# Late norms of a 14-part transformer kernel: the sum of squares moved from GpSimd to VectorE, formed by fp32r products, and placed behind the third weight slab in the FFNs

## The reference

```
y = x * rsqrt(mean(x * x) + 1e-6) * g
x = x + rms_norm(sq_relu_mlp(rms_norm(x, g2), w1, w2), g3)      # mlp
x = x + 0.5 * (silu(h @ w_gate) * (h @ w_up)) @ w_down          # ffn, h = rms_norm(x)
```

## Time and profile before

| what | value |
|---|---|
| median of 3 runs | 2957.7 us (2955.51 to 2959.45) |
| the profiled execution's own time | 2941.98 us |
| its span | 2940.2 us |
| PE busy | 2802.9 us (95%) |
| DVE busy | 1695.6 us (58%) |
| ACT busy | 1352.6 us (46%) |
| POOL busy | 131.6 us (4%), of it L464 54.7 us in 30 operations |
| chain that ended last | PE 86%, ACT 6%, DVE 6%, POOL 1%, issue 1% |
| mean granted TensorE clock | 0.984 |

### The profile page before, as it was taken

One profiled execution on the slowest core, in us unless ns is written; L12 is line 12 of the kernel. 1 busy time (PEld: TensorE's weight loads), 2 busy tenths in 40 slices (PEclk: granted clock), 3 DMA queues, 4 the chain that ended last, 5 costly groups with the idle time before them and its releaser, 6 DMA issues.

```text
span 2940.2 us, 50425 instructions
## 1 busy us (share of the span) xinstructions
PE 2802.9 (95%) x22436; PEld 2707.9 (92%) x22436; DVE 1695.6 (58%) x1997; ACT 1352.6 (46%) x1621; POOL 131.6 (4%) x123
## 2 busy tenths in 40 slices
PE   7999999999998999989999999899999999799998
PEld 7888998899997999989999999889999999789998
DVE  6766644465465654865655654754664654755564
ACT  4634534454436543553544445454544444454443
POOL 1200000000000000200000000000000000000000
PEclk9999999999999999999999999899999999899999
DMA  6402554355442554511555655324665655324563
GB/s 188 152 20 73 189 185 134 110 158 186 158 158 72 169 190 129 158 58 44 158 187 155 190 187 166 108 87 144 180 188 178 187 187 162 97 95 163 159 200 115
DMA packets 426633, 427.95 MB, mean 146 GB/s; under 512 B 8275, under 2 KB 397761, under 8 KB 426289
## 3 DMA queue, kind: packets, MB, share of 16 engines
q1 hardware_dynamic: 426064, 424.37, 46.2%
q0 software_dynamic: 352, 0.36, 0.1%
HBM read 423.65 MB, written 1.05 MB: 144 GB/s over the span
## 4 chain that ended last, share of the span: by engine, by line
PE 86%; ACT 6%; DVE 6%; POOL 1%; issue 1%; DMA 0%; SPq 0%; POOLq 0%; ACTq 0%; DVEq 0%
PE ps L476 85%; ACT wH L1189 2%; DVE hL L1726 1%; DVE wL L1702 1%; POOL sq L464 1%; PE ps L819 1%; DVE sq L1753 1%; DVE xT L1756 1%; ACT hidden_parts L1233 1%; DMA ring<-in_gdn_w_in 0%; ACT L1202 0%; ACT sq L1228 0%; PE ps L957 0%; DVE hidden_parts L1726 0%; DVE arena L2170 0%
## 5 line engine op out<-in xcount | busy, mean ns | idle before, releaser
L1702 DVE TENSOR_TENSOR wL<-ring,wH 128x2048 fp32r<-128x2048 f32 x400 | 916.9, 2292 | 876.7 <-ACT wH L1189 876.2
L1189 ACT ACTIVATE wH<-ring 128x2048 fp32r<-128x2048 f32 x400 | 766.7, 1917 | 1203.4 <-PE ps L476 1187.2
L476 PE MATMUL ps<-hidden_parts,wH 128*128 128x256 f32 x6784 | 1031.6, 280 | 8.2 <-ACT hidden_parts L1233 3.1
L476 PEld LDWEIGHTS ps<-hidden_parts,wH 128*128 128x128 f32 x6784 | 930.9, 189 | 11.9 <-issue 4.3
L476 PE MATMUL ps<-hidden_parts,wL 128*128 128x256 f32 x3392 | 712.0, 280 | 0.3 <-DVE wL L1702 0.2
L476 PEld LDWEIGHTS ps<-hidden_parts,wL 128*128 128x128 f32 x3392 | 535.9, 189 | 0.7 <-DVE wL L1702 0.7
L476 PE MATMUL ps<-hH,wH 128*128 128x256 f32 x2624 | 377.3, 286 | 8.8 <-ACT hH L1223 4.7
L476 PE MATMUL ps<-hL,wH 128*128 128x256 f32 x2624 | 357.8, 283 | 10.0 <-DVE hL L1726 10.0
L476 PE MATMUL ps<-hH,wL 128*128 128x256 f32 x2624 | 361.5, 279 | 1.6 <-DVE wL L1702 1.6
L476 PEld LDWEIGHTS ps<-hH,wH 128*128 128x128 f32 x2624 | 336.7, 191 | 23.0 <-issue 22.0
L476 PEld LDWEIGHTS ps<-hL,wH 128*128 128x128 f32 x2624 | 331.7, 192 | 11.6 <-DVE hL L1726 11.6
(11 more groups left out here) (262 smaller groups left out, 2030.6 us busy)
## 6 DMA issues: line engine op xcount, KB each, us to landing
ring<-in_mlp_w SPq DMA_DIRECT2D x128, 1024.0 KB, 5.3
ring<-in_ffn_w_gate SPq DMA_DIRECT2D x88, 512.0 KB, 4.0
ring<-in_ffn_w_up SPq DMA_DIRECT2D x88, 512.0 KB, 5.3
ring<-in_ffn_w_down SPq DMA_DIRECT2D x44, 1024.0 KB, 4.9
ring<-in_gdn_w_in SPq DMA_DIRECT2D x32, 1024.0 KB, 5.6
ring<-in_w_in SPq DMA_DIRECT2D x28, 1024.0 KB, 5.3
ring<-in_mlstm_w_in SPq DMA_DIRECT2D x12, 1024.0 KB, 5.3
ring<-in_diff_w_in SPq DMA_DIRECT2D x12, 1024.0 KB, 5.1
```

Of the source, the lines that this page charges most:

```text
L476: return pe.matmul(o, l, r, start=start, stop=stop, **k)
L1189: f(wH[:, n % PARTS, :], ring[:, n % RING, :], ACT.Copy).then_inc(sem("high_split"), 1)
L1702: tt(wL[:, n % PARTS, :], ring[:, n % RING, :], wH[:, n % PARTS, :].bitcast(F32), ALU.subtract)\
```

## The change

GpSimd's three additions go. DVE makes them, in `late_low`, behind its low split of slab 1, each waiting for the one before; then it splits the sum into fp32r halves `sumH`, `sumL` (two operations of 256 columns), laid into chunks 8 and 9 of the low hidden half. TensorE forms the sum over the partitions with two fp32r products. `ones` becomes an fp32r tile, filled by a memset of `rs_mem` and a copy on GpSimd at the start. In the MLP the floor is split likewise: ACT copies the high half behind the last hidden group, DVE subtracts the low half, TensorE adds two fp32r products. In the FFN `summed_norm` stands behind slab 2 (the third slab) and no longer behind `first_products`.

```diff
@@ gpsimd, start and loop over the parts
-            pool.memset(ones[:, :], 1.0)
+            W.chain(pool.memset(rs_mem[:, :], 1.0))
+            pool.tensor_copy(onesR[:, :], rs_mem[:, :])
...
-                if kind in LATE:
-                    pool.wait_ge(sem("xsq_ready"), W.next("xsq_ready", 4))
-                    for n in (4, 2, 1):
-                        ins = pool.tensor_tensor(sq[:, 0:n, :], sq[:, 0:n, :], sq[:, n:2 * n, :], ALU.add)
-                        if n > 1:
-                            W.chain(ins)
-                    ins.then_inc(sem("xsq_summed"), 1)
@@ tensor
                 pe.wait_ge(sem("xsq_summed"), W.next("xsq_summed"))
-                mm(ps[:, bank, 0:T], ones[:, 0:P], sq[:, 0, :], True, True).then_inc(sem("ss_ready"), 1)
+                for b, part in enumerate((sumH, sumL)):
+                    last = mm(ps[:, bank, 0:T], onesR[:, 0:P], part, b == 0, b == 1)
+                last.then_inc(sem("ss_ready"), 1)
...
-                pe.wait_ge(sem("floor_set"), W.next("floor_set"))
-                mm(ps[:, bank, 0:T], ones[:, 0:P], rs[:, :], True, False, skip_group_check=True)
+                pe.wait_ge(sem("floor_split"), W.next("floor_split"))
+                for b, part in enumerate((floorH, floorL)):
+                    mm(ps[:, bank, 0:T], onesR[:, 0:P], part, b == 0, False, skip_group_check=True)
...
             def ffn(kind, l):
                 first_products(kind, l, (0, 1), 2 * DC, lambda w, k, half: w[:, half * DC + k, :], src=ffn_x,
                                together=(kind, l) == ("ffn1", 0))
-                summed_norm()
                 for n in range(2, 22):
...
                     last.then_inc(sem("products_done"), 1)
+                    if n == 2:
+                        summed_norm()
@@ scalar, mlp
-                f(rs[:, :], ps[:, 2, 0:T], ACT.Square, scale=FLOOR / D, bias=bcast[:, 36:37])\
-                    .then_inc(sem("floor_set"), 1)
+                f(rs[:, :], ps[:, 2, 0:T], ACT.Square, scale=FLOOR / D, bias=bcast[:, 36:37])
...
                 hidden_high(15)
+                f(floorH, rs[:, :], ACT.Copy).then_inc(sem("floor_set"), 1)
@@ vector, late_low and mlp
                 split(slab_no[(name, layer, 0)] + PARTS)
+                dve.wait_ge(sem("xsq_ready"), W.next("xsq_ready", 4))
+                for n in (4, 2, 1):
+                    W.chain(tt(sq[:, 0:n, :], sq[:, 0:n, :], sq[:, n:2 * n, :], ALU.add))
+                W.chain(dve.tensor_copy(sumH, sq[:, 0, :]))
+                tt(sumL, sq[:, 0, :], sumH.bitcast(F32), ALU.subtract).then_inc(sem("xsq_summed"), 1)
...
                 hidden_low(15)
+                dve.wait_ge(sem("floor_set"), W.next("floor_set"))
+                tt(floorL, rs[:, :], floorH.bitcast(F32), ALU.subtract).then_inc(sem("floor_split"), 1)
```

More of the change, by code:

```diff
@@ L139 @@
           "gates_in", "first_gates_in", "conv_in", "pads_zero",
-          "hs_ready", "hrs_ready", "score_done", "max_ready", "prob_turned", "probT_ready", "xsq_ready", "xsq_summed")
+          "hs_ready", "hrs_ready", "score_done", "max_ready", "prob_turned", "probT_ready", "xsq_ready", "xsq_summed", "floor_split")
 VECTOR_SETUP = {"lambda_sums": 1, "lb_diff": 2, "lambda_ready": 3, "lb_ready": 4, "params_ready": 5}
@@ L222, in program @@
         const = sb("const", [P, NCONST])
-        ones = sb("ones", [P, T])
+        onesR = sb("onesR", [P, T], F32R)
+        ones = onesR.bitcast(F32)
         epsc = sb("epsc", [P, 1])
@@ L315, in program @@
         lwork = arena[0:1, 600:732]
+        sumH, sumL = hidL[:, 8, :], hidL[:, 9, :]
+        floorH, floorL = hH[:, 0, :], hL[:, 0, :]
         x_rows = sq[:, :, :].rearrange("p c t -> p (c t)").rearrange("p (i n) -> p i n", i=TT)
```

## The result

The changed kernel takes 2918.2 us (median of 4 runs, 2915.2 to 2921.4), the kernel before on the same chip 2957.3 (4 runs): ratio 0.9875, 95% interval 0.9854 to 0.9896. The forecast was 2955.2 with a range of 2947 to 2964: wrong, by 37 us, on the side of faster. The profiled execution took 2915.2 us, span 2913.5, against a span of 2940.2 before; mean granted clock 0.984 in both. So the profiles differ by 26.7 us, the medians by 39.

The account below looks back on a forecast made before the run. The prediction took TensorE to bound the kernel (86% of the span). Its terms, -14.4 - 0.85 - 1.55 + 8.7 + 5.6 = -2.5 us, took the median of 2957.7 to 2955.2 us, range 2947 to 2964.

Parts of the forecast that it names:

- MLP, -14.4: Four MLPs: with GpSimd's additions gone, hL and later splits end earlier; gains 3.7, 3.4, 3.7 and 3.6 us.
- the hold of hL: After an MLP's kind of norm: GpSimd's additions hold DVE's eight hL operations, 6.86 us instead of 3.28.
- the rival on the slower side: MLPs and first FFN: hL stays held by ACT's work, not GpSimd's additions; +14.6 us, 2972.3; chance 0.10.
- Adding on DVE, 3.3 us: Late norms: DVE's chain of additions and sum split takes 3.3 us with hand-overs, bounds 2.6 to 3.9.
- FFN, +8.7: Four FFNs: the sum behind the third slab makes TensorE stand 3.6 us for slab 3's low split; +8.7 us together.
- clock, +5.6: Behind each of the four new FFN stalls TensorE falls to half clock, 1.4 us each; bounds 0 and 6.8.
- Cross, -1.55: Two cross attentions: TensorE is free of the 1.36 us wait for GpSimd; -1.5 us in the first, -0.05 in the second.
- Dearer table load: Rival at the FFN stalls: ACT's table load out of idling takes 1.28 us longer; +5.1 us, 2960.3; chance 0.04.
- The floor, -0.85, and the sums' type: Four MLP floors: two fp32r products (0.24 us) replace fp32 (0.45 us), 0.21 us saved each; sums priced likewise.
- The ten sums are inside the other terms: Ten late norms: the sums' change to fp32r products got no separate term.
- 5.66 us (48 x 0.118) for a slab: FFN working: each slab of 48 products was taken to last 5.66 us on TensorE.

Follow-up runs that it names:

- e1: Changed kernel with the FFN's sum product back behind the first two slabs: 2896.7 us, ratio to the kernel before 0.9829.
- e15: The kernel of e1 again, on another chip: 2893.6 us, ratio to the kernel before 0.9832.
- e13: Changed kernel with only the floor's product fp32 again: 2922.7 us, ratio to the kernel before 0.9931.
- e11: The kernel of e1 with one fp32r product of ones with ones as filler at 16 places: 2903.0 us, ratio to the kernel before 0.9888.
- e14: Kernel before with sum and floor each one fp32r product from high halves, GpSimd still adding, places as before: 2912.4 us, ratio 0.989.
- e5: Changed kernel unaltered, timed again on another chip: 2918.9 us, ratio to the kernel before 0.9899.
- e8: Changed kernel with one fp32r product of ones with ones at 104 places in the MLPs' slabs: 2925.1 us (one execution).
- e4: Kernel before with the additions on DVE; products of sum and floor fp32, the FFN's sum in its old place: 2911.0 us, ratio 0.9877.
- e7: Changed kernel with one fp32 product of ones with ones at 104 places in the MLPs' slabs: 2975.1 us (one execution).
- e12: Changed kernel with four fp32 products in a row at the 104 places of e7: 3096.4 us (one execution).

## Why the prediction was wrong

The steps, by the time from the start of a part's first slab to that of its sixth:

- *MLP, -14.4.* Before 33.5, 33.3, 33.5, 33.5 us, after 29.4, 28.8, 28.8, 29.4: together -17.4. In the first and fourth, at the slow rate in both kernels, 4.1 was won for 3.7 and 3.6 forecast. The mechanism (the hold of hL goes with GpSimd's additions) was right, and the rival on the slower side is refuted by the longest hL of 481 ns. The rule of the Trainium skill's GPSIMD Engine Reference, section Specifications, stood the test here: by it the hold had to go, and it went.
- *Adding on DVE, 3.3 us.* Measured 3.19 with the copy at 0.29 us, where I had taken 0.35.
- *FFN, +8.7, and clock, +5.6.* The four grew by 2.6, 5.3, 4.1 and 4.6 us, 16.6 together for 14.3. The stall is 3.54 us for 3.6. A fall was taken at 1.4 us; three of the four half-clock stretches lasted 6.8 us, which is 3.4 us each. e1 and e15 show the price of the move from the other side: 23 to 24.5 us of span, with the 1.36 us waits for GpSimd gone as well.
- *Cross, -1.55.* -1.8 in the first (forecast -1.5), +0.3 in the second (-0.05), where TensorE's wait for ACT at the key product grew from 0.26 to 2.02 us, as forecast in kind.
- *Dearer table load.* It did not come: 1.28 us out of idling, the next operation at 2243.72, 0.01 us later. The drain of the Trainium skill's ScalarE: Activation LUTs, section What ACT_TABLE_LOAD costs, is not seen here either.
- *The floor, -0.85, and the sums' type: the step that failed.* It prices the type by the product's own time alone, "0.45 us each" as fp32 against "0.24 us" for two fp32r products, and says "The ten sums are inside the other terms". That time is right and beside the point. What the type can decide is the rate of the some 700 products behind it: 4.44 ns each, 3.2 us for half an MLP (170.76 against 167.56 in e13). With it falls the premise under every sum of mine, "5.66 us (48 x 0.118) for a slab", as if a slab had one length: it is 5.44 (48 x 0.1133) or 5.65 (48 x 0.1178). I took the slow one, and took it for granted on both sides.

The two errors by the traces: the terms of the forecast together gave -3.0 us for -2.5; the term that was missing gave -23.7. That the first two lie so close is partly luck: the MLPs won 3.0 us more than forecast, the FFNs and their clock cost 2.3 more. The medians are a further 12 us apart that the two profiled executions don't explain. That before was profiled in an execution 16 us under its median, after in one at the low end of its four, accounts for it arithmetically; whether those 16 us were slow products too is open, since the timed executions have no trace here.

**Shown:** that a single fp32 product of 256 columns between fp32r products ended the quick rate each time (quick to slow at 55 of the 55 interruptions without a wait in the traces of e1 to e11, e13, e14 and before; never kept), that fp32r products kept it (180 of 180), that the types alone give the change's ratio (e14), that the late FFN sum costs (e1, e15 against e5). **Only argued:** that all of the rate's 23.7 us comes from the types. In the FFNs the changed kernel's sum has no wait in front of it, and quick stayed quick behind all four, as in e8. In the MLPs the change did two things at once: the sum's product became fp32r, and it now stands behind a wait of 0.46 us. Behind that wait the stream came up slow in two of after's four MLPs with fp32r products, and quick in all four of e4's with fp32 ones, so there the type of the sum isn't what decided; that of the floor, which has no wait, is shown by e13. e4, with fp32 products, also reached 0.9877, by another sum: no stalls, and 9.2 us of rate. **Open:** what the two rates are; what a wait or a late start of 30 to 90 ns does to the rate, since the stream behind one comes up at either; why a product of 512 columns can leave the quick rate standing; what orders slow, slow, slow, quick in e7, as e12 refuted my counter.

## What to carry to other kernels

Before pricing an edit on a TensorE-bound kernel, compare long runs of equal products without a wait (the chain of waits has their length and count): if ns per product differ by a few per cent, there is a term that no wait shows, and it may outweigh all others. Keep a lone fp32 product out of a stream of fp32r ones, test such an edit with the product's type alone, and take several traces, since the rate of a stretch can differ between two executions of one kernel (e1, e15). And a wait for a helper engine is better cured by giving its work to an engine with idle time (1.2% with products and places as before, e4) than by a later place of what waits, which gave 0.5 to 0.7% back (after and e5 against e1).

## What the runs showed of the hardware

- Equal 128x256 fp32r products issued every 113.3 or 117.8 ns at the full granted clock, each rate held for up to a whole part. A single fp32 product of 256 columns (0.45 us) turned quick into slow at 55 of 55 places, and slow into quick at 26 of e7's 78; one of 512 columns kept quick at 13 of 42.
- The DVE operation L1726 (128x256, two SBUF inputs) took 477 ns, with GpSimd adding up to 2603; with GpSimd silent none of 32 is above 481.
- An fp32 to fp32r copy of 128x256 on DVE took 0.29 us, the subtraction beside it 0.43.
- In after, the four TensorE waits of 3.5 us were each followed by a stretch at half clock, three of them of 6.8 us.
